# Sums of squares of attention heads: one fp32 product per pair, or two rounded ones half a body later

## The reference

```python
def rms_norm_2(x, g):
    xf = x.astype(jnp.float32)
    y = xf * lax.rsqrt(jnp.mean(xf * xf, axis=-1, keepdims=True) + RMS_EPS)
    return (y * g.astype(jnp.float32)).astype(x.dtype)

dq = apply_rope(rms_norm_2(dq.reshape(gshape), dil_q_norm), cos, sin)   # likewise dk, fq, fk
```

## Time and profile before

| | |
|---|---|
| median of 3 runs | 3419.26 us (3418.97 to 3421.07) |
| the profiled execution, its own time | 3422.76 us |
| its span | 3421.0 us |
| PE busy | 3386.0 us, 99% |
| DVE busy | 2239.6 us, 65% |
| ACT busy | 1726.5 us, 50% |
| POOL busy | 567.5 us, 17% |
| stretch of bodies 1 to 20 of `w_in_2` | about 1967 to 2202 us of the span |

### The profile page before, as it was taken

The page is one execution under the profiler, slowest core; times in us unless marked ns, Lnnn a source line. Parts: engine busy times, 40 slices in busy tenths (PEclk is TensorE's granted clock), DMA queues, the critical chain, the costliest instruction groups (busy, mean ns, idle before and its releaser), DMA issues.

```text
span 3421.0 us, 58873 instructions
## 1 busy us (share of the span) xinstructions
PE 3386.0 (99%) x19482; PEld 2947.6 (86%) x19482; DVE 2239.6 (65%) x2932; ACT 1726.5 (50%) x2550; POOL 567.5 (17%) x510
## 2 busy tenths in 40 slices
PE   8999999999999999999999999999999999999999
PEld 7898878888888878888888888888888888888888
DVE  7868677777754475655655588856687655555544
ACT  5545565555544454454444444454566545445433
POOL 1204111111100011111100057711100111111000
PEclk9999999999999999999999999999999999999999
DMA  6434545555566645555566655554556555555665
GB/s 203 161 99 136 185 150 186 187 191 186 187 190 186 191 148 190 189 187 188 185 189 188 212 170 172 186 171 155 170 190 199 184 191 189 184 192 188 185 191 171
DMA packets 175310, 616.09 MB, mean 180 GB/s; under 512 B 20833, under 2 KB 21249, under 8 KB 174849
## 3 DMA queue, kind: packets, MB, share of 16 engines
q1 hardware_dynamic: 174800, 609.84, 55.1%
q10 hardware_dynamic: 432, 5.24, 0.4%
HBM read 610.81 MB, written 4.19 MB: 180 GB/s over the span
## 4 chain that ended last, share of the span: by engine, by line
PE 87%; DVE 9%; issue 1%; ACT 1%; DMA 1%; POOL 0%; SPq 0%; DVEq 0%; ACTq 0%; POOLq 0%
PE acc L348 56%; PE acc L351 28%; DVE weights_low L274 3%; DVE x_T L2452 1%; DVE x_T L2450 0%; DVE arena L2456 0%; PE ps_narrow L2194 0%; PE ps_wide L2170 0%; DVE x_T L2454 0%; DVE moving_halves L574 0%; DVE arena L421 0%; DVE x_T L2460 0%; DVE x_T L677 0%; DVE x_T L2444 0%; PE ps_wide L1322 0%
## 5 line engine op out<-in xcount | busy, mean ns | idle before, releaser
L348 PE MATMUL acc<-moving_halves,weights_high 128*128 128x512 f32 x6400 | 2046.3, 400 | 4.8 <-DVE weights_low L274 4.0
L274 DVE TENSOR_TENSOR weights_low<-weights_raw,weights_high 128x1024 fp32r<-128x1024 f32 (+1 forms) x1184 | 1435.7, 1227 | 736.6 <-ACT weights_high L267 735.0
L267 ACT ACTIVATE weights_high<-weights_raw 128x1024 fp32r<-128x1024 f32 (+1 forms) x1184 | 1220.8, 1033 | 792.1 <-PE acc L351 770.2
L351 PEld LDWEIGHTS acc<-moving_halves,weights_low 128*128 128x128 f32 x6400 | 1204.1, 188 | 284.2
L351 PE MATMUL acc<-moving_halves,weights_low 128*128 128x256 f32 x6400 | 1259.1, 278 | 0.0
L348 PEld LDWEIGHTS acc<-moving_halves,weights_high 128*128 128x128 f32 x6400 | 981.5, 189 | 23.1 <-issue 15.9
L348 PE MATMUL acc<-gated_halves,weights_high 128*128 128x512 f32 x2112 | 663.3, 395 | 0.0
L415 ACT ACTIVATE cross_products<-acc 128x256 f32<-128x256 f32 x512 | 196.0, 383 | 690.7 <-PE acc L351 690.6
L351 PEld LDWEIGHTS acc<-gated_halves,weights_low 128*128 128x128 f32 x2112 | 396.7, 188 | 93.8
L438 POOL TENSOR_TENSOR stage_scratch<-unscaled,token_scale 128x256 f32<-128x256 f32 x264 | 219.5, 831 | 1287.8 <-DVE unscaled L421 785.8
L351 PE MATMUL acc<-gated_halves,weights_low 128*128 128x256 f32 x2112 | 414.9, 278 | 0.0
(11 more groups left out here) (340 smaller groups left out, 1840.5 us busy)
## 6 DMA issues: line engine op xcount, KB each, us to landing
weights_raw<-in_w_in SPq DMA_DIRECT2D x272, 512.0 KB, 3.9
weights_raw<-in_ffn_up SPq DMA_DIRECT2D x176, 512.0 KB, 4.0
weights_raw<-in_ffn_w_gate SPq DMA_DIRECT2D x176, 512.0 KB, 3.7
weights_raw<-in_ffn_w_up SPq DMA_DIRECT2D x176, 512.0 KB, 4.3
weights_raw<-in_ffn_w_down SPq DMA_DIRECT2D x160, 512.0 KB, 3.9
weights_raw<-in_ffn_down SPq DMA_DIRECT2D x80, 512.0 KB, 4.1
weights_raw<-in_w_out SPq DMA_DIRECT2D x64, 512.0 KB, 3.7
weights_raw<-in_ffn_w_down SPq DMA_DIRECT2D x32, 256.0 KB, 2.7
```

The source lines that it names most:

```text
L267: core.nc.scalar.activation(core.high[:, slot, 0:nk, :].rearrange("p a b -> p (a b)"), core.raw[:, slot, 0:nk * P], ACT.Copy).then_inc(cor ...
L274: core.nc.vector.tensor_tensor(core.low[:, slot, 0:nk, :].rearrange("p a b -> p (a b)"), core.raw[:, slot, 0:nk * P], core.high[:, slot, 0 ...
L348: core.nc.tensor.matmul(acc[:, t % 2, :, :], core.high[:, u % SLOTS, k, :], parts[:, prod.first[t] + k0 + k, :, :], start=(k0 + k == 0), s ...
L351: core.last = core.nc.tensor.matmul(acc[:, t % 2, 0, :], core.low[:, u % SLOTS, k, :], parts[:, prod.first[t] + k0 + k, 0, :], start=False ...
```

## The change

The sum of squares of a pair is made of two products in float32r, of its high and its low part, instead of one in fp32, and most steps move by half a body:

- ACT writes the squares twice at t = 0 (`head_squares`): once in fp32, once rounded to float32r. It also copies the ones once into a float32r tile. The root that body i made at t = 1 is now made at t = 0 of body i+1 (`head_root(i)`), in front of that body's squares.
- DVE has a new operation, `squares_low`: fp32 squares minus rounded squares, 128x512, directly behind the take of tile 0. `variance` is now behind the take of tile 1, and `normalize` is in the next body, behind split 0 and ahead of the take of tile 0.
- PE multiplies after tile 1 of the body, waits for the low squares, and makes two products of 512 columns.
- The wait of ACT for the last turn and the load of the masks move one body later.

```diff
@@ scalar
+        nc.scalar.activation(ones, core.c("ones"), ACT.Copy).then_inc(squared, 1)
+        def head_root(i):
+            act.wait_ge(var_ready, i)
+            act.wait_ge(normed, i)
+            core.carry_wait(act)
+            nc.scalar.activation(root, var, ACT.Abs_reciprocal_sqrt).then_inc(rooted, 1)
+
+        def head_squares(i):
+            taken(core, act, prod, i - 1, 1)
+            nc.scalar.activation(sq, pair(i - 1), ACT.Square).then_inc(squared, 1)
+            nc.scalar.activation(sq_high, pair(i - 1), ACT.Square).then_inc(squared, 1)
...
         for i, t in walk(2, 1 + QK_BODIES):
-            head_step(i, t)
+            if t == 0:
+                head_root(i - 1)
+                head_squares(i)
             take_cross(core, act, prod, acc, i, t)
         for i, t in walk(1 + QK_BODIES, 2 + QK_BODIES):
+            if t == 0:
+                head_root(i - 1)
+            value_step(i, t)
+            take_cross(core, act, prod, acc, i, t)
+        for i, t in walk(2 + QK_BODIES, 3 + QK_BODIES):
             if t == 1:
                 act.wait_ge(rotated, QK_BODIES + 1)
                 attention.load_masks(act)
@@ vector
+        def squares_low(i):
+            dve.wait_ge(squared, i * 2 + 1)
+            nc.vector.tensor_tensor(sq_low, sq, sq_high.bitcast(F32), ALU.subtract).then_inc(own, 1)
...
         for body in range(1, QK_BODIES):
             for i, t in walk(body, body + 1):
-                if t == 1:
-                    variance(i)
-                take_head(i, t)
-                if t == 1:
-                    normalize(i)
+                if t == 0 and body > 1:
+                    normalize(i - 1)
+                take_head(i, t)
+                if t == 0:
+                    squares_low(i)
+                else:
+                    variance(i)
@@ tensor
         for i, t in pe_steps(core, pe, prod, acc, 1, 1 + QK_BODIES):
-            if t == 0:
-                pe.wait_ge(squared, i)
-                nc.tensor.matmul(p_sq[:, :, :], core.c("ones"), sq, start=True, stop=True).then_inc(summed, 1)
+            if t == 1:
+                pe.wait_ge(own, i * 4 - 3)
+                nc.tensor.matmul(p_sq[:, :, :], ones, sq_high, start=True, stop=False)
+                nc.tensor.matmul(p_sq[:, :, :], ones, sq_low, start=False, stop=True).then_inc(summed, 1)
```

More of the change, by code:

```diff
@@ L141, in __init__ @@
         self.h_at = nc.sbuf_base
+        self.x_at = self.h_at - KT * S * 4
         self.h_mem = self.sb("halves_memory", [P, KT, 2, S], F32)
@@ L2349, in mix_in_stage @@
     var, tmp, swap, root, sq = (core.x[:, 2 * j:2 * j + 2, :] for j in (1, 2, 3, 5, 6))
+    sq_high, sq_low, ones = (core.over(core.x_at + 4 * S * j, name, 1)[:, 0, :, :] for j, name in (
+        (0, "head_squares_high"), (12, "head_squares_low"), (14, "ones_high")))
+    ones = ones[:, 0, 0:P]
     token_eps = core.total[:, :]
@@ L2383, in scalar @@
         act.wait_ge(kept, 16)
-        def head_step(i, t):
-            if t == 0:
[L2387 to L2393, removed]
+        nc.scalar.activation(ones, core.c("ones"), ACT.Copy).then_inc(squared, 1)
[8 more added lines that the diff above has]
+            nc.scalar.activation(sq_high, pair(i - 1), ACT.Square).then_inc(squared, 1)
         def value_step(i, t):
@@ L2413, in scalar @@
             take_cross(core, act, prod, acc, i, t)
-        for i, t in walk(2 + QK_BODIES, FIRST):
+        for i, t in walk(3 + QK_BODIES, FIRST):
             value_step(i, t)
@@ L2450, in normalize @@
             nc.vector.tensor_tensor(tmp, root, root, ALU.mult).then_inc(own, 1)
-            dve.wait_ge(own, i * 3 - 2)
+            dve.wait_ge(own, i * 4 - 2)
             nc.vector.scalar_tensor_tensor(tmp, tmp, -0.5, var, ALU.mult, ALU.mult).then_inc(own, 1)
-            dve.wait_ge(own, i * 3 - 1)
+            dve.wait_ge(own, i * 4 - 1)
             nc.vector.scalar_tensor_tensor(root, tmp, 1.5, root, ALU.add, ALU.mult).then_inc(own, 1)
-            dve.wait_ge(own, i * 3)
+            dve.wait_ge(own, i * 4)
             nc.vector.scalar_tensor_tensor(here, here, core.v("head_gain", i - 1), root, ALU.mult, ALU.mult).then_inc(normed, 1)
@@ L2472, in vector @@
             for i, t in walk(body, body + 1):
-                if t == 1:
+                if t == 0 and body > 1:
+                    normalize(i - 1)
+                take_head(i, t)
+                if t == 0:
+                    squares_low(i)
+                else:
                     variance(i)
-                take_head(i, t)
-                if t == 1:
-                    normalize(i)
         for i, t in walk(QK_BODIES, 1 + QK_BODIES):
-            if t == 1:
+            if t == 0:
+                normalize(i - 1)
+            take_for_scaling(core, dve, prod, acc, i, t)
+            if t == 0:
+                squares_low(i)
+            else:
                 variance(i)
+        for i, t in walk(1 + QK_BODIES, 2 + QK_BODIES):
+            if t == 0:
+                normalize(i - 1)
             take_for_scaling(core, dve, prod, acc, i, t)
-            if t == 1:
-                normalize(i)
-        for i, t in walk(1 + QK_BODIES, FIRST):
+        for i, t in walk(2 + QK_BODIES, FIRST):
             take_for_scaling(core, dve, prod, acc, i, t)
```

1 line of the change is left out of this document (removed).

## The result

| | before | after |
|---|---|---|
| median of 6 runs | 3420.14 us (3418.97 to 3423.93) | 3431.39 us (3429.63 to 3434.11) |
| ratio | | 1.0033, 95% interval 1.0023 to 1.0044 |
| profiled execution, its own time | 3422.76 us | 3429.63 us |

The changed kernel is slower by 11.3 us. The two profiled executions differ by 6.9 us only, so the stage has to be measured by itself. I take it from the sum of the tokens' squares ahead of it, in PE's timeline after and before,

What follows compares the result with a forecast made beforehand. PE, 99% busy, was taken as the bound, with DVE overtaking it after the change. Bodies -0.7 and +7.3, end +2.1, +0.4, +0.7 make +9.8, taken as +9.2: 3432.0 profiled, 3428.5 us median, range 3424.5 to 3433.

Steps and rivals of the forecast that it cites:

- PE's part: PE's own work per body: two rounded products take 0.47 us instead of 0.82, body 11.62 us, 0.35 less.
- ACT's part: One more square on ACT, 0.61 us per body, with the cross half's copy still in time: costed at nothing.
- DVE's part: DVE per body: 10.19 us of its own plus two turn operations' standstill, 2.0 us; the followed-through cycle closes at 12.40 us.
- the case that the prediction set aside in brackets: POOL's first turn operation gets in beside the short take, so the subtraction stands still instead; same sum.
- The sum for the bodies: Query and key bodies: -0.7 us for two on DVE's reserve, then +7.3 us for 17 at 12.40 instead of 11.97.
- the reserve: DVE's time in hand at the start of the stretch, expected to keep PE from waiting for two bodies.
- The end: End of the stretch: +2.1 us for the last variance, +0.4 for body 20, +0.7 for the transposes' waits.
- The late variance: Before body 21 PE waits 2.8 us for the last variance, where it waited 0.63 before: +2.1 us.
- The transposes: In bodies 21 and 22 PE's transposes wait for POOL's scaling, two waits of about 1 us: +0.7 us.
- the saving arrives: Rival: DVE needs 11.44 us and fits into 11.62, giving -4 us (3415) or -7 (3412); chance 0.18.
- the rounded products cost two passes: Rival on PE: 1.64 us in place of 0.82, body 12.8 us, 3439 us; within the worse outcomes, chance 0.08 together.
- the rule: Turn operations enter only at DVE waits or long PSUM reads, run 1.0 us, and block DVE operations with two SBUF inputs.

Runs made afterwards that it cites:

- e3: Changed kernel with GpSimd's three turn operations cut to 4 of 256 columns, for measuring only: 3411.92 us, ratio 0.9977 to the kernel before.
- e8: Changed kernel with fp32 squares in PSUM, two end waits moved and the root's square made by ACT instead of DVE: 3410.20 us, ratio 0.9969 to before.
- e4: Changed kernel with the fp32 squares in PSUM instead of SBUF, same operations, order and waits: 3422.71 us, ratio 1.0007 to the kernel before.
- e2: Changed kernel without DVE's subtraction, both rounded products reading the high part: 3421.85 us, ratio 1.0004 to the kernel before.
- e1: Changed kernel's new order alone, with one fp32 product, no rounded squares and no subtraction: 3424.20 us, ratio 1.0011 to the kernel before.

## Why the prediction held, step by step

The forecast was +9.2 us, 3428.5 in a range of 3424.5 to 3433, and the mechanism a wait of PE for the low squares, caused by turn operations on shared ports. It measured +11.3 and 3431.39, by this mechanism. That the sum came out so near is in part luck: the bodies were 1.9 us more than forecast and the end about 0.9 less, and which operations would stand still was wrong.

- **PE's part.** Two products 0.46 us, body 11.62: right. The first body with the new products lasts 11.64 (1968.69 to 1980.33), e3's and e8's 11.60. Where PE has waited the pair costs 0.57 (start 2068.12, next product 2068.69), 0.1 more than I had.
- **ACT's part** at nothing: right, no engine waits for its squares or cross halves in the bodies.
- **DVE's part.** 10.19 us of its own and 2.0 us of standstill: both right (2.0 us as read above). The body came out at 12.54 and not 12.40, since split 0 starts 4.80 us behind the end of the low squares (2068.07 to 2072.87) and not 4.65 (the terms given there add up to 4.62); 0.1 of it is the longer products, and the gap ahead of split 0 grows by the same amount, to 0.3 us. Where the standstill falls I had wrong: not on split 0 and L2470 but on the low squares (1.10), split 3 (0.17) and split 0 (0.71). It is the case that the prediction set aside in brackets, with the same sum, as it said.
- **The sum for the bodies.** +6.6 for bodies 1 to 19, measured +8.5. The 0.14 us per body over 17 bodies make +2.4, and the reserve lasted for one body instead of two, +0.9; the mean body before is 12.01 and not 11.97, -0.7, and body 20 was 0.7 shorter, since its low squares ran free. This is the mis-sized term.
- **The end.** The late variance: a wait of 2.8 expected, 2.42 measured. The low squares of body 20 missed the standstill, as they had in the body at 2128.95; what decided it the starts don't show, as is told below. The transposes: +0.7 expected, +0.85 measured (2.1 for 1.25), in one wait and not two. ACT's wait of 6.2 us is gone.
- **The rivals.** That the saving arrives needs the ports free: e3 shows that it would arrive, 8.0 us by the medians, where I had priced it at 4 to 7. That the rounded products cost two passes is excluded by the 0.23 us between them.
- **Where the rule failed.** "A turn operation gets in only where DVE waits or does something long that reads PSUM" fits the body of the kernel before that it was read from. In the changed kernel the first turn operation got in at the short take of tile 0, ahead of the low squares, in 17 of 19 bodies, which the prediction allowed for in its brackets only. In e4 the second turn operation got in between two splits in a row, and in e2 one after a single split. The moment of the start doesn't explain it: the first turn operation starts 0.17 or 0.18 us behind that take in every body, in the 17 and in the two where it lost, and in e1 too, where splits follow the take and it lost in all 20. What decides this order stays open; it was worth 0.4 to 0.7 us per body and made me expect too much of e2 and e4.
- **What the expectations of e2 and e4 left out.** They had no term for PE's clock. None was needed for the changed kernel, but in e2 and e4 the lower clock behind the long wait made up about 1.6 and 1.7 us of the misses.

## What to carry to other kernels

A saving on the busiest engine is worth what the next one can follow, and here that next limit was not VectorE's work (10.2 of 11.6 us) but its work plus the GpSimd operations that shut it out: add both up before adding an operation with two SBUF inputs. A wait of VectorE may be where the other engine's work is hidden; an order that closes it gives the standstill back elsewhere. Cheap ways out were an operand in PSUM and an operation moved to ScalarE: together with an end of the stretch in which no engine waits behind a turn, the same idea went from +11.3 to -10.0 us. And a long wait of TensorE can cost more than its length: the one of 4.2 us in e4 cost about 5.9 with the slow steps behind it.

## What the runs showed of the hardware

A VectorE operation with two SBUF inputs and a GpSimd operation exclude each other for about 1.0 to 1.1 us per 32x512 operation; with one input in PSUM (e4's low squares, 0.67 us beside L2553) they run side by side. Which of the two gets the ports where both ask is not told by the starts: with the same 0.17 to 0.18 us between the start of the take and its own, the first turn operation won in 17 of 19 bodies of the changed kernel and in none of 20 in e1. TensorE's granted clock was 1.00 through its waits of 4.2 us (e4) and 3.4 us (e2), and 0.50 in a stretch behind them; a pair of steps then took 1.28 us instead of 0.70.
